# Two chained decoder blocks on one core: state outputs of the RWKV blocks in column halves, a norm's rate in three steps, the step sizes' softplus in later rounds, and the convolution split into lagged parts

## Chip, cores and metric

One core of a Trainium2 chip runs the whole program. The metric is the device time of one execution in microseconds (us). Engines are named as in the profile: PE (TensorE, matmuls; PEld is its loading of weights), DVE (VectorE), ACT (ScalarE), POOL (GpSimd), SP (SyncE, which issues the weight DMAs).

## What is computed

The reference runs two blocks behind each other on x of 256 tokens by 2048 features, all in float32. The change touches the second block's mixer alone:

```
u = rms_norm(h, norm1_g)                 # h is the first block's output after its final norm
P = u @ w_in                             # z, xbc, dt_raw, and the RWKV part pr
pr = pr + (prev - pr) * mu               # token shift
y_ssd:  xbc = silu(causal_depthwise_conv(xbc, w[4], b)); dt = softplus(dt_raw + dt_bias)
        chunked state space scan over x, B, C with dt and A
y_rwkv: S_t = S_{t-1} * w_t + (S a_t) b_t + v_t k_t ;  y_t = S_t r_t   per head of 64
h = h + concat(y_ssd, y_rwkv) @ w_out
```

There are 32 heads of 64 for each of the two mixers, so two heads share the 128 partitions. The convolution runs over 24 tiles of 128 channels (16 of x, 8 of B and C).

## The kernel before

Activations lie feature-major: a tile is 128 features by T = 256 tokens. Every large matrix product (`linear`) reads weights as float32 from HBM in pieces of 128x1024. ACT copies a piece to its rounded high part (L2036), DVE subtracts for the low part (L1199), and PE runs three matmuls for each 128x128 block (hi by hi, hi by lo, lo by hi: L703, L704, L705). Four buffers hold cut pieces. A tile of the second block's input projection has 16 blocks, hence two pieces.

Every engine runs a program of its own, in order. All are written by generators of the same shape, and the order is set by hand by where they `yield`. `second_mixer` makes rounds: in each round `main` advances by 5 yields (5 of a tile's 16 blocks), and then each of the other generators by one yield, in the order heads of even number (`heads(0)`), of odd number (`heads(1)`), `tails`, `afters`, and those of `early`. `AFTER, PAIRS, ROUNDS = 25, 56, 20` say in which round the pair's preparation begins, in which the first blocks begin, and how many rounds lie between pairs.

- `main` runs `L_sm` (4 tiles: decay, a and gate low-rank parts, and dt), then eight groups of `L_krv` (6 tiles each: k, r, v of a pair of head tiles), from the fifth on with a small gate product `L_g2` in between, then `L_bc` (8 tiles) and `L_x` (6 and 10 tiles), whose tiles go through the convolution. DVE's `raw_shift` takes a tile out of its bank (L1615), ACT scales it (L2274), DVE adds the shifted part (L1625).
- `both_rates` is in `early`. DVE makes the rate of the first block's final norm and of the second block's first norm in one round (L1259 to L1270, two reciprocals among them), ACT takes the roots (L2523, L2524). DVE then scales h in eight rounds (L1277); ACT stores h (L2528) 13 rounds in and eight rounds later loads `w2` and `a2` (L2532, L2533) into h's place.
- `steps_dt`, also in `early`, is the softplus of dt and its running sum on 32 partitions: L1646 to L1680 on DVE, two `Exp` on ACT (L2297, L2300). Its temporaries are the scratch tiles `scr[0:4]`, which `prep` uses afterwards; ACT's `prep(0)` and `prep(1)` therefore wait for its end (`dt_v["cs"]`).
- `after(b)` is `prep` of two head tiles side by side (`flight`), one `yield`, and `solve(b)`: PE multiplies (L933), DVE sorts the result with eight instructions (L1752) and transposes (L1756), and POOL inverts the 32x32 triangles by 31 pairs of instructions (L2710, L2714). DVE's `finish(b)` (L1735, L1737) waits for POOL; it is called by `solve(b+1)` or by the first block that needs it.
- `block(i, hf)` takes ten rounds: transposes (L948 to L951), masks (L958, L960 on PE, L1774 on DVE), L965, L972, then L978 to L984, L990 with L1795 on DVE, and four chunks of 32 tokens, one for each round. A chunk waits for the state of the one before (DVE L1802, ACT L2376), adds its output to bank A by one matmul with the 128x128 block-diagonal state, 32 columns wide (L1002), and makes the next state by six matmuls of 64 output columns, in pairs for the two heads (L1006, L1008, L1011). The two heads' results go to the two halves of the partitions, `HALVES`.
- `tail(i)` is the group norm of a finished head tile; it waits for `solve` to have left banks 2 and 3 (`wkv_v["xa", ...]`).
- `conv4(t)`, in `main`: DVE takes the tile out of its bank (L1851), ACT makes bias plus last tap (L2400), DVE adds three taps (L1855, three instructions), ACT applies Silu (L2403), all for the same t. Ahead of `L_bc` ACT waits until the gated output of pair 4 is stored (L2394, semaphore `st_y[1]`).

`Lag(L, f0, f1, ...)` is a helper that calls at tile t the parts in the order f_n(t - n), ..., f1(t - 1), f0(t); `tail()` runs what is left over. `timed((n, g))` starts g after n rounds.

## Time and profile before

| | |
|---|---|
| median of 3 runs | 3125.03 us (3124.04 to 3125.74) |
| the profiled execution: time | 3126.62 us |
| its span on the core | 3124.5 us |
| PE busy | 2925.9 us, 94% |
| DVE, ACT, POOL busy | 2132.1, 1559.1, 714.7 us |
| mean granted clock of PE | 0.978 |

The time and the span of the profiled execution differ by 2.1 us. "Busy" is the union of an engine's instructions; matmuls overlap, so PE's progress is better read from the starts of its instructions. The second mixer's rounds lie between about 1184 and 2035 us of the span.

### The profile page before, as it was taken

The numbers are of one execution on the slowest core, as the hardware profiler recorded it, in microseconds if no ns is written. First come the engines' busy times: TensorE is split into PE (matmuls) and PEld (weight loads), VectorE is DVE, ScalarE is ACT, GpSimd is POOL, SyncE is SP. The second block draws the span as 40 slices with busy tenths as digits, with TensorE's granted clock in tenths as the row PEclk, the third lists the DMA queues.
The fourth block names the chain that finished last, engine by engine and source line by source line (L and its number), as shares of the span: only waits on it lengthen the run. The fifth ranks groups of instructions, "written<-read, shape, count | busy, mean of one in ns | idle before, by whom it ended". The sixth has DMA issues, their size and how long they took to land. (4 is left out here: it accounts for less than half of the span.)

```text
span 3124.5 us, 51838 instructions
## 1 busy us (share of the span) xinstructions
PE 2925.9 (94%) x20742; PEld 2613.5 (84%) x20742; DVE 2132.1 (68%) x3449; ACT 1559.1 (50%) x2582; POOL 714.7 (23%) x885
## 2 busy tenths in 40 slices
PE   4976999999999998899999989998999999999998
PEld 4865998888888887888888778987888888888887
DVE  7787887775777657677777666666756665566655
ACT  3445555553555544455555555455444444444443
POOL 5256402210111100565555440000100110001100
PEclk9987999999999999999999999999999999999999
DMA  4420555556555555322222222344455555655554
GB/s 179 166 68 26 164 177 190 192 173 193 206 191 189 166 173 184 132 96 89 89 89 89 88 76 93 134 165 148 163 176 182 191 192 171 195 201 189 185 176 138
DMA packets 78958, 475.30 MB, mean 152 GB/s; under 512 B 8128, under 2 KB 11200, under 8 KB 37440
## 3 DMA queue, kind: packets, MB, share of 16 engines
q1 hardware_dynamic: 76480, 459.66, 43.1%
q10 hardware_dynamic: 2240, 12.32, 1.1%
q8 instruction: 167, 2.74, 0.4%
q14 instruction: 71, 0.58, 0.1%
HBM read 465.66 MB, written 6.29 MB: 151 GB/s over the span
## 5 line engine op out<-in xcount | busy, mean ns | idle before, releaser
L705 PE MATMUL bank<-m,m 128*128 128x256 f32 x6864 | 1931.6, 281 | 0.0
L701 PE MATMUL bank<-m,m 128*128 128x512 f32 x4736 | 1658.3, 394 | 5.3 <-DVE m L1945 2.8
L1199 DVE TENSOR_TENSOR m<-m,m 128x1024 fp32r<-128x1024 f32 (+1 forms) x944 | 1079.5, 1151 | 605.8 <-ACT m L2036 599.8
L705 PEld LDWEIGHTS bank<-m,m 128*128 128x128 f32 x6864 | 1302.1, 190 | 1.2
L2036 ACT ACTIVATE m<-m 128x1024 fp32r<-128x1024 f32 (+1 forms) x944 | 911.5, 979 | 719.8 <-PE bank L705 701.0
L701 PEld LDWEIGHTS bank<-m,m 128*128 128x128 f32 x4736 | 890.5, 188 | 204.0 <-issue 5.6
L703 PE MATMUL bank<-m,m 128*128 128x256 f32 x2128 | 639.8, 301 | 66.8 <-DVE m L1199 60.5
L704 PE MATMUL bank<-m,m 128*128 128x256 f32 x2128 | 606.5, 285 | 0.0
L703 PEld LDWEIGHTS bank<-m,m 128*128 128x128 f32 x2128 | 411.3, 193 | 96.3 <-issue 79.6
L704 PEld LDWEIGHTS bank<-m,m 128*128 128x128 f32 x2128 | 411.8, 193 | 1.8
L2691 POOL TENSOR_TENSOR m<-m,m 128x256 fp32r<-128x256 f32 x44 | 63.4, 1441 | 690.1 <-ACT m L2258 690.1
L2714 POOL TENSOR_TENSOR m<-m,m 128x31 f32<-128x31 f32 (+15 forms) x248 | 167.5, 675 | 19.5
L2710 POOL TENSOR_TENSOR m<-m,m 128x31 f32<-128x31 f32 (+15 forms) x248 | 161.3, 651 | 19.4
L2682 POOL TENSOR_TENSOR m<-m 128x256 f32<-128x256 f32 x44 | 32.6, 742 | 447.3 <-DVE m L1587 447.3
L2274 ACT ACTIVATE m<-m,m 128x256 f32<-128x256 f32 (+1 forms) x52 | 26.5, 509 | 140.9 <-DVE m L1615 140.9
L2241 ACT ACTIVATE m<-bank 128x256 f32<-128x256 f32 x88 | 34.1, 387 | 116.2 <-PE bank L705 116.1
L2685 POOL TENSOR_TENSOR m<-m,m 128x256 fp32r<-128x256 f32 x44 | 63.4, 1441 | 123.2 <-ACT m L2235 123.2
L2771 POOL TENSOR_TENSOR m<-m,m 128x256 fp32r<-128x256 f32 x8 | 7.5, 968 | 328.0 <-ACT m L2460 328.0
L717 PE MATMUL bank<-m,m 128*128 128x256 f32 x236 | 65.0, 389 | 11.7 <-ACT m L2058 11.3
L1592 DVE TENSOR_TENSOR m<-m,bank 128x256 f32<-128x256 f32 x88 | 37.1, 421 | 56.6 <-ACT m L2241 56.6
L2215 ACT ACTIVATE m<-bank 128x256 f32<-128x256 f32 x88 | 34.0, 386 | 74.9 <-PE bank L705 74.9
L2376 ACT ACTIVATE m<-bank,m 64x64 f32<-64x64 f32 x128 | 39.5, 308 | 52.4 <-PE bank L1011 40.8
(368 smaller groups left out, 2929.2 us busy)
## 6 DMA issues: line engine op xcount, KB each, us to landing
m<-in_w_up SPq DMA_DIRECT2D x88, 1024.0 KB, 4.8
m<-in_w_down SPq DMA_DIRECT2D x128, 704.0 KB, 4.1
m<-in_w_gu SPq DMA_DIRECT2D x88, 1024.0 KB, 4.8
m<-in_w_out SPq DMA_DIRECT2D x48, 1024.0 KB, 5.1
m<-in_w_krv SPq DMA_DIRECT2D x48, 1024.0 KB, 4.8
m<-in_w_xbc SPq DMA_DIRECT2D x24, 1024.0 KB, 4.8
m<-in_w_z SPq DMA_DIRECT2D x16, 1024.0 KB, 4.8
m<-in_w_in SPq DMA_DIRECT2D x14, 1024.0 KB, 4.8
```

The costliest lines, as they stand in the source:

```text
L701: pe.matmul(bank.rearrange("p (a b) -> p a b", a=2), hi, x, start=kc == L.k0, stop=False)
L703: pe.matmul(ps, hi, x[:, 0, :], start=kc == L.k0, stop=False)
L704: pe.matmul(ps, hi, x[:, 1, :], start=False, stop=False)
L705: m = pe.matmul(ps, lo, x[:, 0, :], start=False, stop=last)
L717: pe.matmul(banks[N.bank][:, 0:T], ones, square_of(N, i), start=i == 0, stop=i == N.nk - 1).then_inc(*norm_pe(("sq", q)))
L1199: v.tensor_tensor(lo_of(k), raw_of(k)[0], hi_of(k).bitcast(F32), SUB).then_inc(*lo_v(("lo", k)))
L2036: a.activation(hi_of(k), src, ACT.Copy).then_inc(*hi_a(("hi", k)))
L2376: a.activation(sn[R, R], bB[R, R], ACT.Copy, scale=PL[R, i, hf * 4 + c:hf * 4 + c + 1]).then_inc(*wkv_a(("s", i, hf, c)))
L2685: g.tensor_tensor(far[:, 1, j % 22, :], s[:, 1, :], far[:, 0, j % 22, :].bitcast(F32), SUB).then_inc(*ffn_g(("lo", j)))
L2691: g.tensor_tensor(far[:, 1, j % 22, :], cvs2[j % 4], far[:, 0, j % 22, :].bitcast(F32), SUB).then_inc(*ffn_g(("lo2", j)))
L2710: g.tensor_tensor(prod, XB[:, r + 1:32, r:r + 1].broadcast_to([128, n, r + 1]), XX[:, r:r + 1, 0:r + 1].broadcast_to([128, n, r + 1]), MUL ...
L2714: g.tensor_tensor(x5, x5, prod, ADD).then_inc(*wkv_g(*([("x", b)] if r == 30 else [])))
```

## The change

- PE's L1002 becomes two matmuls, for the 64 state columns of each head, which write the two halves of bank A's partitions.
- `both_rates` is spread over three rounds on DVE; on ACT it begins two rounds later, and its counts of rounds behind are one lower, so that the store of h and the loads of `w2`, `a2` come one round later.
- `steps_dt` begins in round 31 (`STEPS = 30`), with h's first three tiles as temporaries (partitions 96 to 128, once h is stored) and its input in `dt_`; ACT's `prep(0)` and `prep(1)` no longer wait for it.
- `after(b)` has one more `yield` ahead of `solve(b)` on every engine.
- The convolution becomes `convolved(L)`: DVE runs `conv4(t-1)` and then `raw4(t)`; ACT runs the Silu of t-2 (`gated`) and then bias and last tap of t (`weighted`). The wait for the store of pair 4 moves from the head of `L_bc` to the Silu of tile 22.

```diff
-AFTER, PAIRS, ROUNDS = 25, 56, 20
+AFTER, PAIRS, ROUNDS, STEPS = 25, 56, 20, 30
+        dth = [h[:, n, :] for n in range(3)]
@@ tensor: block
-                        m = pe.matmul(bA[:, Q], sb_, qb[:, Q], start=False, stop=c == 3)
+                        for R in HALVES:
+                            m = pe.matmul(bA[R, Q], sb_[:, R], qb[:, Q], start=False, stop=c == 3)
@@ after(b), on all four engines
                 yield from flight(lambda i: prep(2 * b + i), 2, 2)
                 yield
+                yield
                 yield from solve(b)
@@ vector: both_rates
                 v.reciprocal(rr, ms).then_inc(*norm_v())
+                yield
...
-                v.reciprocal(ms, rl).then_inc(*norm_v())
-                v.wait_ge(*norm_v.last)
+                v.reciprocal(ms, rl).then_inc(*norm_v(("rm",)))
+                yield
+                v.wait_ge(*norm_v["rm"])
@@ vector: steps_dt
-                a, e, w, p = (q[R, :] for q in scr[0:4])
-                for _ in range(5):
-                    yield
+                a, e, w, p = (q[R, :] for q in (dt_, *dth))
+                v.wait_ge(st_h, 16)
@@ vector: convolution
+            def raw4(t):
...
+            def conv4(t):
+                s, ps = cvb[t % 2], shp[t % 2]
+                v.wait_ge(*ssd_v["raw", t])
                 v.wait_ge(*ssd_a["id", t])
...
+            def convolved(L):
+                steps = Lag(L, raw4, conv4)
+                yield from linear(L, steps)
+                steps.tail()
@@ scalar: prep
-                a.wait_ge(*(wkv_v["prep", i - 2] if i >= 2 else dt_v["cs"]))
+                if i >= 2:
+                    a.wait_ge(*wkv_v["prep", i - 2])
@@ scalar: convolution
+            def convolved(L, dst):
+                def weighted(t):
                     a.wait_ge(*ssd_v["raw", t])
...
+                def gated(t):
+                    if t == 22:
+                        a.wait_ge(st_y[4 % 3], 16 * (4 // 3 + 1))
                     a.wait_ge(*ssd_v["conv", t])
-                    a.activation(dst(t), s, ACT.Silu).then_inc(*ssd_a(("conv", t)))
-                return done
+                    a.activation(dst(t), cvb[t % 2], ACT.Silu).then_inc(*ssd_a(("conv", t)))
+
+                steps = Lag(L, weighted, lambda t: None, gated)
@@ scalar: main
-                a.wait_ge(st_y[4 % 3], 16 * (4 // 3 + 1))
@@ scalar: both_rates
+                yield
+                yield
                 a.wait_ge(*norm_v["rc", N_two.id])
...
-                for _ in range(12):
+                for _ in range(11):
                     yield
@@ vector and scalar
-            second_mixer(main(), block, tail, after, steps_dt(), both_rates(...), ...)
+            second_mixer(main(), block, tail, after, timed((STEPS, steps_dt())), both_rates(...), ...)
```

## Rows read from the trace of the kernel before

**Rows 1.** Page, part 1: busy time, share of the span, instructions.
```profile
PE 2925.9 (94%) x20742; PEld 2613.5 (84%) x20742; DVE 2132.1 (68%) x3449; ACT 1559.1 (50%) x2582; POOL 714.7 (23%) x885
```
**Rows 2.** Windows of the second mixer's stages: length, busy by engine, granted clock, DMA.
```profile
1180.00:1247.00 67.00, 53.46 (x401) 51.71 (x400) 52.06 (x90) 30.28 (x43) 5.95 (x11) 0.95 0.49 168
1247.00:1334.00 87.00, 71.66 (x583) 69.28 (x582) 61.89 (x108) 41.17 (x64) 48.52 (x67) 0.94 0.36 131
1334.00:1757.00 423.00, 410.19 (x4037) 365.24 (x4035) 295.64 (x605) 242.40 (x489) 248.08 (x382) 0.98 0.27 91
1757.00:1965.00 208.00, 186.60 (x1808) 165.88 (x1809) 133.23 (x268) 112.12 (x210) 41.12 (x64) 0.96 0.26 88
```
**Rows 3.** Windows at one stall of PE and just behind it.
```profile
1464.00:1466.00 2.00, 0.32 (x3) 0.11 (x2) 1.97 (x5) 0.00 (x0) 0.00 (x0) 1.00 0.00 0
1466.80:1470.20 3.40, 3.40 (x18) 3.40 (x17) 2.60 (x5) 2.04 (x4) 0.00 (x0) 0.50 0.85 308
```
**Rows 4.** Timeline of ACT in the opening: start, length, instruction, idle before.
```profile
1189.99 0.42 ACT L2523 ACTIVATE m<-m 128x256 f32<-128x256 f32 x1 [4.66 <-DVE m L1270]
```
**Rows 5.** Timeline of DVE in the opening.
```profile
1191.70 1.23 DVE L1199 TENSOR_TENSOR m<-m,m 128x1024 fp32r<-128x1024 f32 x1 [1.74 <-ACT m L2036]
```
**Rows 6.** Timeline of PE in the opening.
```profile
1193.07 0.36 PE L703 MATMUL bank<-m,m 128*128 128x256 f32 x1 [1.70 <-DVE m L1199]
```
**Rows 7.** Groups of DVE, 1184.7 to 1240: busy, mean ns, idle before.
```profile
L1666 DVE TENSOR_TENSOR m<-m,m 32x256 f32<-32x256 f32 x8 | 3.4, 422 | 0.3
L1668 DVE TENSOR_SCALAR m<-m 32x256 f32<-32x256 f32 x8 | 3.3, 409 | 0.3
```
**Rows 8.** DMA issues, 1220 to 1250: size, us to landing.
```profile
m<-in_a ACTq DMA_DIRECT2D x1, 768.0 KB, 9.0
```
**Rows 9.** Timeline of POOL, begin of `solve(0)`.
```profile
1274.85 0.95 POOL L2703 MEMSET m<- 128x1024 f32 x1 [45.53 <-DVE m L1756]
```
**Rows 10.** Timeline of DVE where it takes up `solve(0)`'s result.
```profile
1326.51 1.25 DVE L1735 STREAM_TRANSPOSE m<-m 128x1024 f32<-128x1024 f32 x1 [4.04 <-POOL m L2714]
```
**Rows 11.** POOL's 31 additions, 1274 to 1327.
```profile
L2714 POOL TENSOR_TENSOR m<-m,m 128x31 f32<-128x31 f32 (+15 forms) x31 | 23.8, 768 | 2.4
```
**Rows 12.** The same, 1477 to 1524.
```profile
L2714 POOL TENSOR_TENSOR m<-m,m 128x31 f32<-128x31 f32 (+15 forms) x31 | 19.4, 627 | 2.4
```
**Rows 13.** Timeline of PE: a first chunk, which has no L1002.
```profile
1348.64 0.28 PE L705 MATMUL bank<-m,m 128*128 128x256 f32 x1
...
1349.01 0.29 PE L1008 MATMUL bank<-m,m 128*64 128x64 f32 x4
```
**Rows 14.** Timeline of PE: a chunk with L1002 behind a linear block.
```profile
1623.83 0.28 PE L705 MATMUL bank<-m,m 128*128 128x256 f32 x1
...
1624.37 0.29 PE L1008 MATMUL bank<-m,m 128*64 128x64 f32 x4
1624.48 0.29 PE L1011 MATMUL bank<-m,m 128*64 128x64 f32 x4
```
**Rows 15.** Timeline of PE: a chunk with L1002 behind matmuls of half width.
```profile
1378.92 0.44 PE L984 MATMUL bank<-m,m 128*64 128x128 f32 x4
...
1379.79 0.29 PE L1008 MATMUL bank<-m,m 128*64 128x64 f32 x4
```
**Rows 16.** Timeline of DVE around `solve(3)`.
```profile
1473.37 2.53 DVE L1752 TENSOR_TENSOR m<-bank,m 32x128 f32<-32x128 f32 x8
...
1480.10 0.87 DVE L1795 TENSOR_TENSOR m<-bank,m 64x256 f32<-64x256 f32 x2
```
**Rows 17.** Timeline of PE, the chunk that needs this L1795.
```profile
1482.68 0.41 PE L1002 MATMUL bank<-m,m 128*128 128x32 f32 x2
```
**Rows 18.** Timeline of ACT at the head of `L_bc`.
```profile
1767.60 1.06 ACT L2036 ACTIVATE m<-m 128x1024 fp32r<-128x1024 f32 x1 [5.20 <-DMA ysave<-m]
```
**Rows 19.** Groups of ACT, 1761 to 2030.
```profile
L2403 ACT ACTIVATE m<-m 128x256 f32<-128x256 f32 x24 | 10.0, 418 | 31.8 <-DVE m L1855 31.8
```
**Rows 20.** Groups of DVE, 1761 to 2030.
```profile
L1855 DVE SCALAR_TENSOR_TENSOR m<-m,m,m 128x255 f32<-128x255 f32 (+2 forms) x72 | 35.9, 499 | 20.6 <-ACT m L2400 18.9
```

More of the change, by code:

```diff
@@ L1839, in gated @@
                 v.tensor_tensor(VV(t), VV(t), bank_of(L_g2[t // 2], t), MUL).then_inc(*wkv_v(("gate", t)))
-            def conv4(t):
-                s, ps = cvb[t % 2], shp[t % 2]
+            def raw4(t):
+                ps = shp[t % 2]
                 L = L_x[t >= 6] if t < 16 else L_bc
@@ L1866, in main @@
                 yield from linear(L_g2[4], gated)
-                yield from linear(L_bc, conv4)
+                yield from convolved(L_bc)
                 yield from linear(L_g2[5], gated)
                 for k in range(2):
-                    yield from linear(L_x[k], conv4)
+                    yield from convolved(L_x[k])
                     yield from linear(L_g2[6 + k], gated)
@@ L1996, in vector_program @@
             v.tensor_scalar(omka, WR("rwkv_k_a_2"), -1.0, 1.0, MUL, ADD).then_inc(*once_v(("omka",)))
-            second_mixer(main(), block, tail, after, steps_dt(), both_rates(ffn_v.last),
+            second_mixer(main(), block, tail, after, timed((STEPS, steps_dt())), both_rates(ffn_v.last),
                          timed((CLOSING, chain(turn_dt(), turn_cb(), turn_x(0, 13)))))
@@ L2293, in steps_dt @@
                 R = slice(96, 128)
-                for _ in range(5):
-                    yield
+                yield
                 a.wait_ge(*dt_v["w"])
-                a.activation(scr[1][R, :], scr[2][R, :], ACT.Exp).then_inc(*dt_a(("e",)))
+                a.activation(dth[0][R, :], dth[1][R, :], ACT.Exp).then_inc(*dt_a(("e",)))
                 for _ in range(6):
@@ L2417, in main @@
                 a.wait_ge(*wkv_v["out", 9])
-                a.wait_ge(st_y[4 % 3], 16 * (4 // 3 + 1))
-                yield from linear(L_bc, conv4(L_bc, lambda t: bc[:, t - 16, :]))
+                yield from convolved(L_bc, lambda t: bc[:, t - 16, :])
                 yield from gated(5)
@@ L2422, in main @@
                 for k in range(2):
-                    yield from linear(L_x[k], conv4(L_x[k], lambda t: xT[:, t, :]))
+                    yield from convolved(L_x[k], lambda t: xT[:, t, :])
                     yield from gated(6 + k)
@@ L2427, in after @@
                 yield from flight(lambda i: prep(2 * b + i), 2, 2)
+                yield
                 yield
@@ L2521, in both_rates @@
             def both_rates():
+                yield
+                yield
                 a.wait_ge(*norm_v["rc", N_two.id])
@@ L2533, in both_rates @@
                 a.dma_start(a2s[0:96, :], d["a2"]).then_inc(ld_a2, 16)
-            second_mixer(main(), block, tail, after, steps_dt(), both_rates())
+            second_mixer(main(), block, tail, after, timed((STEPS, steps_dt())), both_rates())
             last_mixer(chain(linear(L_z, z_done), linear(L_outr, lambda t: None)), quad, iter(range(3)), norm_ssd,
@@ L2744, in after @@
                 yield from flight(lambda i: iter(range(7)), 2, 2)
+                yield
                 yield
```

14 lines of the change are left out of this document (8 added, 6 removed).

## Prediction

> **What bounds the kernel now.** I began with the page's busy shares [rows 1]: PE works 94% of the span, so an edit counts only if it shortens PE's own work or one of PE's waits. Then I cut the span into windows. In the two feed-forward parts PE is busy throughout; PE's idle time lies in the mixers, and the change touches the second one. There [rows 2] PE idles 67.0 - 53.5 = 13.5 us in the opening (1180 to 1247), 87.0 - 71.7 = 15.3 us up to the first blocks (to 1334), 12.8 us in the 423 us of steady rounds, and 21.4 us in the 208 us in which the convolution runs beside the last blocks. The same rows show a second price: the granted clock's mean is 0.94 to 0.98. [rows 3] show how that comes: PE, at 2.4 GHz, works 0.32 of 2 us, and in the 3.4 us from its restart it is granted 0.50, the level of 1.2 GHz. So such a stall costs 3.4 x 0.5 = 1.7 us more. Over rows 2 the lost clock is 0.05 x 67 + 0.06 x 87 + 0.02 x 423 + 0.04 x 208 = 25 us. In all, 63 us of idling and 25 us of clock can be had or made worse.
>
> **Opening: the rate in three rounds, softplus out of the way.** Now ACT sits 4.66 us in front of its root, waiting for DVE's six instructions [rows 4], and only then copies the next piece; DVE cuts it at 1191.70 [rows 5], and PE waits 1.70 us for it [rows 6]. After the change ACT copies that piece first, and DVE cuts it right behind its second reciprocal, about 1189.5: this stall goes. The root is needed for the first tile all the same and comes only 1.1 us earlier, so most of the next stall stays. Behind it DVE has 12.7 us of softplus between the cuts: eight pairs of 3.4 + 3.3 us [rows 7] and some 6 us of single instructions. I walked through the 26 rounds with those gone, a tile being 16 x 3 matmuls at 0.118 us = 5.7 us of PE: three stalls remain, each where ACT changes tables for a Tanh or Sigmoid ahead of a copy. PE is through the second tile at 1194.1, the third's first piece is cut at 1196.6 (2.5 us); through the fourth at 1208.1, with the fifth's piece at 1210.4 (2.3); through the fifth at 1216.1, with the sixth's at 1217.6 (1.5). From there tiles of 5.7 us follow without a stall, and PE reaches round 26 about 12 us earlier, with two half-clock stretches saved.
>
> Not all of it lasts. `w2` and `a2` are asked for one round later while PE arrives earlier; `a2` takes 9.0 us to land [rows 8], and from round 22 to round 26 PE needs 4 rounds of 1.8 us = 7.1 us. So PE waits about 2 us where it now waits 0.2. And `solve(0)` on POOL sets the pace next: it begins at 1274.85 [rows 9], ends at 1326.5, 51.7 us later, and DVE waits 4.04 us for it [rows 10], PE 5.5 us. What PE saves between these two points only lengthens that wait. The path is: opening, preparation, `solve(0)`, first blocks. On it are 12 saved, 2 lost to `a2`, 1.8 lost because `solve(0)` begins a round later, 1 for softplus instructions now between preparation and `solve(0)`, and 1.8 won back because `finish(0)` also comes a round later in the program, so that PE has done one more round when it stops. That makes 9. The 7 us of softplus that fall beside POOL's chain are covered by the wait of 4.0 us and by what is left of PE's 4 us wait in front of L933, which the extra yield relieves; without that cover they would cost up to 7.
>
> POOL's chain itself can suffer: its 31 additions take 768 ns each here, but 627 ns beside steady rounds [rows 11, 12], 4 us on the path already. The softplus adds some 7 us to the 62 us in which DVE is busy there [rows 2]; in proportion that is 0.5 us more for POOL, and I count it in the 1 us above. The Trainium skill (SBUF — State Buffer, Terms) says that of DVE and GpSimd the loser blocks for the other's whole instruction; the slower additions agree, and by it alone the eight products of 0.42 us could hold POOL for up to 3.4 us. For the opening: 9 us, from 3 (`a2`'s landing and the bursts at twice their price, little cover left) to 13.
>
> **State outputs in halves.** L1002 is one float32 matmul of two passes with the whole array, amid groups that use it in halves. A chunk without it takes 0.37 us from the last linear matmul to L1008 [rows 13], with it 0.54 [rows 14]. As halves it becomes another pair of groups like its neighbours: L1008 to L1011 is 0.11 us [rows 14], so 0.48, a gain of 0.05 for some 60 chunks, 3 us. Behind L984 [rows 15] the path L984 to L1008 is 0.87 us, because the array changes from halves to whole and back; all in halves it should be 0.22 (L984's four passes of 128 columns, half of them at a time: twice the 0.11 of the 64 columns in [rows 14]) + 0.11 + 0.11 = 0.44. That is 0.42 us for 15 chunks, 6.3 us. The 37 chunks behind other whole-array matmuls gain 0.03 to 0.2 each, 3 us. Together 12 us of PE. Bounds: if the two halves do not run beside each other, the group takes 0.22 instead of 0.11 and 112 chunks give back 12 us, which leaves nothing; if 32 columns take half of what 64 take, 0.055, it is 18 us. PE has short waits on DVE in each period of 20 rounds, and three quarters should come through: 9 us, range 3 to 14.
>
> A rule speaks against it. The Trainium skill (TensorEngine Tiling (Array Packing), Performance Considerations) warns not to take the tiling from a dimension that is already small, as each matmul has some 60 cycles of overhead; 32 moving columns are such a case. No row here has 32 columns in halves. By the page's figure, 25 ns at 2.4 GHz, two more passes in 112 chunks would be an estimated 6 us of cost in place of the gain.
>
> **`solve` a round later, in every period.** Steady rounds do not need it: PE has no stall at L933 there. DVE's burst of transposes and L1752 (about 5.3 us, [rows 16] show its middle) moves from round 95 to 96 of a period, next to the DVE work of round 97. L1795 ended at 1481.0 and PE needed it at 1482.68 [rows 16, 17]; the burst a round later (3.9 us later, minus 1.2 us of cutting that now comes ahead) ends L1795 at about 1482.9. With the tail's square and root behind it I expect 0.5 to 1 us of new waits, six times: 4 us lost, range 0 to 12 (with a stretch of half clock in half of the periods).
>
> **Convolution.** Queued behind ACT's Silu are its copies and the blocks' evacuations. ACT waits 31.8 us for L1855 before 24 Silus, 1.3 each [rows 19], and DVE 18.9 us for ACT before L1855 [rows 20]. After the change both find their input a tile old. The wait for the store, 5.2 us of ACT [rows 18], goes entirely: the Silu of tile 22 comes seven tiles later. That store alone explains two PE stalls of 2.8 and 1.4 us and one stretch of half clock: 5.9 us. The rest of the 21.4 us and of the clock (8 us) is 24 us, mostly PE waiting for ACT behind a Silu. Against it: `conv4(t-1)` now stands ahead of `raw4(t)` on DVE, 3 x 0.5 = 1.5 us, so where DVE is late the tile leaves its bank 1.5 us later and ACT gains 0.9 instead of 2.4 us. I take 60%: 14 us. Bank turnover is safe, as PE has the other bank's tile (5.7 us) in between; the last Silu of each run still waits, three times. Sum 20 us, range 8 to 27.
>
> **Sum.** 9 + 9 - 4 + 20 = 34 us off the profiled execution's 3126.6, 3092.6; the median of the runs is 1.6 lower, so 3091.
>
> **Rivals.**
> - *Given back.* POOL's chain and `a2` take the opening's gain, new waits in the periods take that of the halves, and the convolution yields its lower half: about -14 us, 3111. For it speaks that DVE is busy 62 of 87 us beside POOL [rows 2].
> - *Everything runs.* With stalls gone the clock stays up: 13 + 14 - 0 + 27 = 54 us, 3071. Against it: the burst in `prep` that stalls PE at 1465.9 [rows 3] is untouched.
> - *Small columns.* The halves do not overlap at 32 columns, and the pair of groups costs the 0.22 us of the bound above: the 9 us are gone, 3100. For it: the passes of the two halves are too short to hide each other's weights; against it: the neighbours with 64 columns do [rows 14]. The Trainium skill's tiling rule above is this case.
> - *No effect.* DVE is late in every tile and ACT waits for L1851 as long as it did for L1855; PE's stalls change places. 3122 to 3128.
> - *Slower.* The later burst in `solve` stalls PE not for 0.5 but for 5 us in each of seven periods, and each stall brings a stretch of half clock: 7 x (5 + 1.7) = 47 us against 38 gained, 3134. It decides from 3.7 us of stall per period on, where the 38 us are used up. Against it: the old timeline leaves 1.7 us of room.
>
> **Chances.** As forecast (3078 to 3104) 0.56; given back 0.16; everything 0.10; small columns 0.06; no effect 0.05; slower 0.07. The range that leaves out no more than 2 in 10 is 3074 to 3112; the likeliest case's own is 3078 to 3104. Within 0.2% (6.2 us, about what a measurement of this kernel can tell from no change): 0.05; faster 0.88; slower 0.07.
>
> **What would show it.** In the profile after: ACT's wait in front of L2523 shorter and PE's wait for L1199 in the opening about 6 us in place of 13.5; a wait of some 2 us for `in_a`; DVE's wait for POOL in front of its first L1735; L984 to L1008 at 0.44 us; waits of PE on L1795 near each `solve`; no idle ACT before Silu. Wrong it would be if these DVE bursts stall PE for whole microseconds, or if ACT's wait simply moves to L1851's successor.

## Result and the profile after

The changed kernel takes 3108.84 us (median of 4 runs, 3107.23 to 3113.15) against 3125.39 us before (4 runs). The ratio is 0.9947, with an interval of 0.9936 to 0.9959: 16.5 us faster. The forecast was 34 us, so the direction was right and about half of the gain was missing. Two of the four terms of the sum came out at their number, two did not.

The profiled execution took 3113.15 us, with a span of 3111.1 us. First the stages of the second mixer, as windows of the changed kernel. The columns are those of [rows 2]. The first inner cut lies at the same round as before. The second lies at round 61, where [rows 2] cut at round 58.8, and the last two lie at the same times as before, not at the same rounds.

```profile
1180.00:1236.00 56.00, 52.19 (x409) 51.15 (x408) 39.03 (x63) 27.84 (x39) 5.67 (x11) 0.97 0.61 205
1236.00:1343.00 107.00, 85.50 (x630) 81.00 (x630) 81.22 (x142) 47.62 (x75) 53.75 (x77) 0.90 0.33 116
1343.00:1757.00 414.00, 390.61 (x4071) 345.04 (x4070) 286.02 (x590) 231.84 (x468) 239.31 (x360) 0.98 0.25 88
1757.00:1965.00 208.00, 195.68 (x2040) 174.68 (x2038) 144.09 (x289) 116.40 (x225) 47.87 (x76) 0.97 0.28 99
```

PE's idle time in the opening is 3.8 us in place of 13.5. In the second stage it is 21.5 us at a granted clock of 0.90, where [rows 2] show 15.3 us at 0.94, and where the same rounds before (1247.0 to 1341.2) take 94.2 us in place of 107.2: the gain of the first stage is gone there. In the last row, where the convolution runs, PE is busy 195.7 us in place of 186.6.

To see where time came and went I counted rounds in each trace by the starts of PE's L704 (L703 before), five of them to a round, and took how much sooner than before each kernel reached a round. All values are counted from its own round 1, one profiled execution each:

| kernel | round 26 | 31 | 61 | 78 | 160 | 190 | 220 | last block |
|---|---|---|---|---|---|---|---|---|
| changed | 12.5 | 8.8 | -0.5 | -2.0 | -5.6 | -0.5 | 10.5 | 14.9 |
| changed, no extra yield | 12.3 | 11.5 | 4.3 | 4.7 | 10.3 | 23.4 | 31.3 | 35.9 |
| changed, L1004 whole | 12.7 | 12.4 | 3.8 | 3.8 | -1.6 | 1.7 | 6.1 | 10.6 |
| changed, softplus from round 61 | 12.7 | 12.8 | 11.6 | 2.6 | -0.9 | 5.8 | 13.7 | 18.2 |
| changed, `finish` a round earlier | 12.5 | 12.5 | 4.5 | 5.3 | 2.4 | 13.7 | 20.2 | 24.8 |
| changed, transpose a round later | 12.5 | 11.5 | 2.1 | 0.9 | 6.0 | 18.3 | 26.3 | 31.0 |
| no extra yield, softplus from 45 | 12.5 | 11.2 | 3.5 | 2.4 | 10.5 | 23.6 | 31.5 | 36.0 |
| no extra yield, softplus from 203 | 12.7 | 11.6 | 11.0 | 11.6 | 19.7 | 32.7 | 36.8 | 41.3 |
| before + rates alone | 0.9 | 0.9 | 0.9 | 0.9 | 1.0 | 1.0 | 1.0 | 1.1 |
| before + softplus alone | 9.9 | 3.9 | -5.0 | -5.0 | -3.4 | -0.5 | 0.9 | 1.1 |
| before + halves alone | 0.0 | -0.3 | 0.2 | 0.7 | 6.1 | 7.6 | 12.9 | 13.4 |
| before + yield alone | -0.1 | 0.0 | -1.2 | -1.4 | -8.4 | -12.8 | -12.9 | -12.7 |
| before + convolution alone | -0.1 | -0.5 | 0.1 | 0.1 | 0.3 | 12.1 | 16.4 | 20.9 |

Between rounds 26 and 61 one program does not always take the same time: the changed kernel, the one with a whole L1004 and the one with `finish` moved run the same instructions up to the first blocks, and stand at -0.5, 3.8 and 4.5 in round 61. So a value in column 61 is good to some 4 us, and the changed kernel's own profile shows a poor pass. Most of the difference arises between rounds 26 and 31, where PE waits 2.2 us for the load of `a2` in the changed kernel's pass and 0.2 us or less in the other two (rows below).

**The opening.** The timeline of ACT and of DVE in the changed kernel, and PE's largest stall there:

```profile
1192.43 0.42 ACT L2548 ACTIVATE m<-m 128x256 f32<-128x256 f32 x1 [4.67 <-DVE m L1275]
```
```profile
1190.90 1.16 DVE L1202 TENSOR_TENSOR m<-m,m 128x1024 fp32r<-128x1024 f32 x1
```
```profile
1197.99 0.55 PE L704 MATMUL bank<-m,m 128*128 128x256 f32 x1 [2.29 <-DVE m L1202]
```

ACT's wait did not shrink (4.67 us, [rows 4] 4.66): it only came behind the copy. The cut is at 1190.90 without a wait of its own, and PE's 1.70 us of [rows 6] are gone. PE reaches round 26 12.5 us sooner. The step of the prediction that walked through these rounds said 12.

**What followed the opening.** The load of `a2`, POOL's start of `solve(0)`, and DVE where it takes up the result:

```profile
m<-in_a ACTq DMA_DIRECT2D x1, 768.0 KB, 12.6
```
```profile
1238.76 1.06 PE L908 MATMUL bank<-m,m 96*128 96x256 f32 x2 [2.19 <-DMA m<-in_a]
```
```profile
1275.97 0.95 POOL L2728 MEMSET m<- 128x1024 f32 x1 [54.77 <-DVE m L1760]
```
```profile
1329.24 1.24 DVE L1739 STREAM_TRANSPOSE m<-m 128x1024 f32<-128x1024 f32 x1
```

The wait for `a2` is the 2 us that the step on `a2` gave it, but it costs more than itself. These are rounds 26 to 31 as windows of the changed kernel, of run 11 (the same instructions there) and of run 12:

```profile
1234.63:1250.19 15.56, 13.37 (x93) 12.49 (x92) 6.04 (x14) 8.33 (x15) 0.00 (x0) 0.89 0.59 207
```
```profile
1234.52:1246.45 11.93, 11.69 (x93) 11.30 (x92) 5.98 (x14) 8.10 (x15) 0.00 (x0) 1.00 0.68 255
```
```profile
1234.91:1252.77 17.86, 14.71 (x94) 13.82 (x92) 6.07 (x14) 8.36 (x15) 0.00 (x0) 0.81 0.48 174
```

PE waits 2.2, 0.2 and 3.1 us for `in_a` in them, and the granted clock is 0.89, 1.00 and 0.81. So the wait of 2.2 us costs 3.6 in this pass, before softplus has begun: its first instruction stands at 1254.99, and round 31 begins at 1250.19.

POOL begins at 1275.97, not sooner than the 1274.85 of [rows 9], although PE was 11 us ahead at round 26 by the clock of the two traces. (Round 1 itself begins at 1182.21 here and at 1180.73 before. Counted from there POOL begins at 93.8 us, before at 94.1.) And in front of L1739 there is no wait in brackets, where [rows 10] show 4.04 us for POOL: DVE comes to it late, and the cover on which the step counted is not there.

**State outputs.** Two chunks on PE in the changed kernel, the first behind the half-width L985, the second behind a linear block:

```profile
1382.80 0.44 PE L985 MATMUL bank<-m,m 128*64 128x128 f32 x4
1383.02 0.31 PE L1004 MATMUL bank<-m,m 128*64 128x32 f32 x4
...
1383.25 0.34 PE L1010 MATMUL bank<-m,m 128*64 128x64 f32 x4
```
```profile
1357.63 0.28 PE L706 MATMUL bank<-m,m 128*128 128x256 f32 x1
1357.84 0.31 PE L1004 MATMUL bank<-m,m 128*64 128x32 f32 x4
...
1358.12 0.29 PE L1010 MATMUL bank<-m,m 128*64 128x64 f32 x4
```

L1010 is the old L1008. Behind L985 it starts 0.45 us after it (0.87 in [rows 15], forecast 0.44); behind the linear matmul 0.49 us after (0.54 in [rows 14], forecast 0.48). Over all chunks without a wait in the traces of the kernel before and of run 15, the path from the last matmul ahead of the state output to this one fell by 0.42 us behind L984 (15 chunks), by 0.03 behind a linear matmul (60 chunks), by 0.08 and 0.03 behind L965 and L972 (15 each) and by 0.22 behind L960 (7). That is 11 us of PE, 6.3 of them behind L984.

**Steady rounds.** The chain of the extra yield around `solve(3)` in the changed kernel: DVE's timeline, ACT's, and PE's.

```profile
1481.03 2.52 DVE L1756 TENSOR_TENSOR m<-bank,m 32x128 f32<-32x128 f32 x8
1483.59 1.25 DVE L1760 STREAM_TRANSPOSE m<-m 128x1024 f32<-128x1024 f32 x1
1484.86 0.42 DVE L1620 TENSOR_TENSOR m<-bank,m 128x256 f32<-128x256 f32 x1
```
```profile
1485.32 0.51 ACT L2287 ACTIVATE m<-m,m 128x256 f32<-128x256 f32 x1 [6.29 <-DVE m L1620]
1485.74 1.04 ACT L2049 ACTIVATE m<-m 128x1024 fp32r<-128x1024 f32 x1
1486.81 0.60 ACT L2364 ACTIVATE m<-bank 128x512 f32<-128x512 f32 x1
```
```profile
1487.46 0.49 PE L959 MATMUL bank<-m,m 64*128 64x128 f32 x4 [1.30 <-ACT m L2364]
```

The burst is not what PE waits for. It stands ahead of L1620, which takes a linear tile out of its bank; ACT idles 6.29 us for that tile, and behind it in ACT's order stands L2364, the evacuation of a block's transposes, for which PE waits.

**Convolution.** Groups of DVE and ACT in the changed kernel, 1757 to 2025:

```profile
L1862 DVE SCALAR_TENSOR_TENSOR m<-m,m,m 128x255 f32<-128x255 f32 (+2 forms) x72 | 36.7, 510 | 3.6 <-ACT m L2416 1.8
```
```profile
L2423 ACT ACTIVATE m<-m 128x256 f32<-128x256 f32 x24 | 9.9, 411 | 3.4 <-DVE m L1862 3.1
```

ACT's idle time before Silu fell from 31.8 us to 3.4 [rows 19], DVE's before its three taps from 20.6 to 3.6 [rows 20]. Two further rows of ACT belong to it. The bias and last tap, in the changed kernel and before:

```profile
L2416 ACT ACTIVATE m<-m,m 128x256 f32<-128x256 f32 x24 | 14.4, 601 | 64.3 <-DVE m L1855 64.2
```
```profile
L2400 ACT ACTIVATE m<-m,m 128x256 f32<-128x256 f32 x24 | 14.4, 600 | 48.2 <-DVE m L1851 48.2
```

So 16 of the 28 us came back as a longer wait for the tile to leave its bank. And ACT's loads of its function table ahead of Silu, in the changed kernel and before:

```profile
L2423 ACT ACT_TABLE_LOAD x4 | 5.1, 1283 | 0.1
```
```profile
L2403 ACT ACT_TABLE_LOAD x7 | 9.0, 1283 | 0.1
```

Those ahead of the tails' root (L2399, before L2386) fell from 6 to 3 as well: together 7.7 us less of ACT's own time, which no term of the prediction names.

### The profile page after: what moved, and what is told of

It is laid out like the page before. It is cut to its first block and busy times, and to the rows that moved or that the text cites. A ratio compares the mean times of both kernels' runs of the same rounds, so it can differ in the third digit from the quotient of the medians.

```text
span 3111.1 us, 52307 instructions
## 1 busy us (share of the span) xinstructions
PE 2913.5 (94%) x20966; PEld 2599.6 (84%) x20966; DVE 2131.0 (68%) x3449; ACT 1550.0 (50%) x2575; POOL 717.1 (23%) x885
## 3 DMA queue, kind: packets, MB, share of 16 engines
HBM read 465.66 MB, written 6.29 MB: 152 GB/s over the span
## 5 line engine op out<-in xcount | busy, mean ns | idle before, releaser
L2049 ACT ACTIVATE m<-m 128x1024 fp32r<-128x1024 f32 (+1 forms) x944 | 911.6, 979 | 716.4 <-PE bank L706 701.9
L704 PE MATMUL bank<-m,m 128*128 128x256 f32 x2128 | 640.2, 301 | 61.6 <-DVE m L1202 51.5
L704 PEld LDWEIGHTS bank<-m,m 128*128 128x128 f32 x2128 | 412.5, 194 | 88.4 <-issue 73.6
L2287 ACT ACTIVATE m<-m,m 128x256 f32<-128x256 f32 (+1 forms) x52 | 26.5, 510 | 164.3 <-DVE m L1620 164.3
L718 PE MATMUL bank<-m,m 128*128 128x256 f32 x236 | 64.8, 388 | 11.8 <-ACT m L2071 11.3
L2389 ACT ACTIVATE m<-bank,m 64x64 f32<-64x64 f32 x128 | 39.6, 310 | 51.4 <-PE bank L1013 36.9
```

The source lines that it names most:

```text
L704: pe.matmul(ps, hi, x[:, 0, :], start=kc == L.k0, stop=False)
L718: pe.matmul(banks[N.bank][:, 0:T], ones, square_of(N, i), start=i == 0, stop=i == N.nk - 1).then_inc(*norm_pe(("sq", q)))
L2049: a.activation(hi_of(k), src, ACT.Copy).then_inc(*hi_a(("hi", k)))
L2389: a.activation(sn[R, R], bB[R, R], ACT.Copy, scale=PL[R, i, hf * 4 + c:hf * 4 + c + 1]).then_inc(*wkv_a(("s", i, hf, c)))
```

## Experiments

Each run's own comparison has kernel-before runs on the same chip; their median lay between 3125.8 and 3126.9 us, for the changed kernel's own 3125.39. Differences from the changed kernel are those of the medians as they stand; against their own kernels before they would be up to 1.5 us different. "Theory" and "rival" are those of the expectation above each result.

**1. Without the extra yield.**

```diff
 def after(b):        # on all four engines
     yield from flight(lambda i: prep(2 * b + i), 2, 2)
     yield
-    yield
     yield from solve(b)
```


> The changed kernel without the extra yield in front of solve, on every engine; all else as changed. Theory A (the gain was lost in two places, and this is one): with the yield, DVE's burst of two transposes and eight sorts stands in front of the evacuation L1620, ACT idles 6.3 us in front of L2287, its copy L2364 comes late and PE waits 1.3 us at L959, plus 1.9 us at L1004 behind L1806, some 2.4 us in each of about six periods; without it those waits fall back to about 2.5 us per period and the time falls by 8 to 14 us, to about 3098 us. Rival B (the yield costs what was forecast or less, and the gain of the halves was never there): within 4 us of the changed kernel, 3105 to 3109. Rival C (the yield relieved the first solve, PE at L934, and was worth it): slower than the changed kernel by 2 to 5 us.

3091.58 us, ratio 0.9886 (0.9874 to 0.9899): 17 us faster than the changed kernel. Theory A is right in its place and too low in size: it expected 8 to 14 us, and the waits at L959 below, 8.4 us fewer, are half of what came. The list of PE's waits, of the changed kernel and of this one (us in total, times, longest):

```profile
PE bank L959 <- ACT m L2364: 11.6, 7, 2.8
```
```profile
PE bank L959 <- ACT m L2362: 3.2, 2, 2.3
```

**2. State output whole again.**

```diff
-for R in HALVES:
-    m = pe.matmul(bA[R, Q], sb_[:, R], qb[:, Q], start=False, stop=c == 3)
+m = pe.matmul(bA[:, Q], sb_, qb[:, Q], start=False, stop=c == 3)
```


> The changed kernel with L1004 as one matmul of the whole array again; all else as changed. Theory A (the halves are sized right, 11 us of PE's own time over 112 chunks, and three quarters come through): slower than the changed kernel by 7 to 11 us, 3116 to 3120 us. Rival B (the waits on DVE and ACT in the steady rounds took it all): within 2 us, 3107 to 3111. Rival D (the halves cost, as narrow tiles would): faster than the changed kernel by 2 us or more.

3119.69 us, ratio 0.9975 (0.9966 to 0.9985): 10.9 us slower than the changed kernel (9.7 by the kernels before of each). Theory A; rivals B and D fall.

**3. Softplus in the steady rounds.**

```diff
-AFTER, PAIRS, ROUNDS, STEPS = 25, 56, 20, 30
+AFTER, PAIRS, ROUNDS, STEPS = 25, 56, 20, 60
```


> The changed kernel with STEPS 60 in place of 30: softplus in rounds 61 to 73, where a round takes 3 to 4 us and DVE is idle for about 1 us of each; all else as changed. Theory A (in rounds 31 to 44 DVE is busy without a pause, so the 7 us of softplus and the slowdown beside POOL delay its cuts and evacuations, and PE loses 11 us between round 26 and round 65): 6 to 11 us faster than the changed kernel, about 3100. Rival E (POOL's chain of 51 us sets the end of the first solve whatever DVE does in front of it): within 2 us of the changed kernel. Rival F (softplus is no better in the later rounds, its stalls only move): within 3 us either way, with new waits of PE in rounds 61 to 73.

3111.34 us (3107.22 to 3122.92), ratio 0.9958 (0.9943 to 0.9974), no better than the changed kernel: theory A missed. Its first half holds, as PE reaches round 61 11.6 us ahead. But PE then loses 9.0 us up to round 78, where softplus now stands, at L1004 in

```profile
1344.10 0.31 PE L1004 MATMUL bank<-m,m 128*64 128x32 f32 x4 [1.39 <-DVE m L1806]
```

and others like them. That was rival F. The trace also shows POOL's chain as a limit, rival E's point. POOL begins 11.7 us sooner than in the changed kernel (9.3 when each is counted from its own round 1, of which 3.7 are rounds 26 to 31, with the wait for `a2`, rather than softplus), and now both DVE and PE wait (POOL, then DVE, then PE):

```profile
1264.31 0.96 POOL L2728 MEMSET m<- 128x1024 f32 x1 [45.46 <-DVE m L1760]
```
```profile
1314.85 1.25 DVE L1739 STREAM_TRANSPOSE m<-m 128x1024 f32<-128x1024 f32 x1 [6.33 <-POOL m L2739]
```
```profile
1323.87 1.12 PE L966 MATMUL bank<-m,m 128*128 128x64 f32 x4 [11.24 <-DVE m L1778]
```

**4. Convolution alone**, in the kernel before: the part of the change's diff with `raw4`, `conv4`, `convolved`, `weighted` and `gated`, and nothing else.

> The kernel before with the convolution's parts lagged alone (raw4, conv4 on DVE; bias and Silu on ACT; the wait for the store at tile 22). Theory A (this part gave what was forecast, 19 to 20 us between round 180 and the end): 3103 to 3108 us, 17 to 22 us faster than before, so more than the whole change gives. Rival G (its gain is owed to the other parts, halves above all, which make room on PE): 8 to 13 us faster, 3112 to 3117.

3106.62 us, ratio 0.9933 (0.9921 to 0.9945): 20.0 us faster. Theory A. PE's wait of 2.8 us at L948, which the prediction put down to the store, is not in this trace.

**5. Softplus beside POOL's chain.** Run 1 with `STEPS` 44.

```diff
-AFTER, PAIRS, ROUNDS, STEPS = 25, 56, 20, 30
+AFTER, PAIRS, ROUNDS, STEPS = 25, 56, 20, 44
```


> The changed kernel without the extra yield and with STEPS 44: softplus in rounds 45 to 57, beside POOL's chain of 51 us and nothing of the preparation. The last run with softplus out of rounds 31 to 44 kept PE 18.6 us ahead of before until round 58 and then stood 11.2 us for the first solve, and lost 9 us more in rounds 61 to 78, where softplus was. Theory A (softplus costs PE its full DVE time wherever PE depends on DVE, and is free only where PE must wait for POOL in any case): PE reaches round 61 about 12 to 14 us ahead of before in place of 1.7, and the time is 8 to 12 us under that of the run without the yield, 3080 to 3084 us. Rival E (POOL's chain is slowed by it, or DVE's queue holds back something else that the first blocks need): within 3 us of that run, 3089 to 3094.

3090.19 us, ratio 0.9882 (0.9867 to 0.9898), against 3091.58 in run 1: rival E. POOL does begin early (1263.57), but PE falls from 12.5 us ahead at round 26 to 3.5 at round 61. In the rounds before 45 it keeps its lead (11.2 us in round 31 and in round 45), so the loss lies where softplus is. So also this place, which by the prediction was covered, costs.

**6. Without the series.** Run 1 with the eight pairs L1670, L1672 of softplus left out, so dt is not the softplus of its input.

```diff
 for k in range(7, -1, -1):
-    v.wait_ge(*dt_v.last)
-    v.tensor_tensor(p, p, w, MUL).then_inc(*dt_v())
-    v.wait_ge(*dt_v.last)
-    v.tensor_scalar(p, p, cf[k], None, ADD).then_inc(*dt_v())
     yield
```


> The changed kernel without the extra yield, with the eight pairs of softplus's series left out (so dt is not the reference's): some 6.7 us of DVE's time in rounds 35 to 44 less, all else where it was. Theory A (these instructions, not the rounds to which the rate was spread or the later loads, cost the stretch from round 26 to 58): PE is 8 to 12 us further ahead at round 58 than with them, and the whole is 6 to 11 us faster than the run without the yield, 3081 to 3086. Rival H (the stretch is lost to DVE's normal work, which now starts late against the slowed POOL side, or to the load of a2): under 3 us faster.

3085.53 us, 6.0 us under run 1 by the medians, at the low end of theory A. The two profiles show less: 5.8 against 4.3 us ahead at round 61, 37.4 against 35.9 at the end. Taken alone this run is no more than a hint.

**7. Rates alone**, in the kernel before.

```diff
 v.reciprocal(rr, ms).then_inc(*norm_v())            # DVE, both_rates
+yield
...
-v.reciprocal(ms, rl).then_inc(*norm_v())
-v.wait_ge(*norm_v.last)
+v.reciprocal(ms, rl).then_inc(*norm_v(("rm",)))
+yield
+v.wait_ge(*norm_v["rm"])
```
(and two more yields on ACT ahead of the roots, one less behind them)

> The kernel before with the rates alone spread over three rounds, and the store of h and the loads of w2 and a2 one round later; softplus stays in rounds 6 to 18. Theory A (most of the opening's 12 us came from softplus leaving it; the split saves the stall in front of L1199 at 1193 alone, 1.7 us and its stretch of half clock, and the later load of a2 takes 0 to 2 back): 0 to 3 us faster than before, 3123 to 3127. Rival I (the split itself gave the larger part of the opening): 5 us or more faster.

3125.18 us, ratio 0.9992 (0.9984 to 1.0001): 1.7 us, theory A, though no change at all is inside the interval too.

**8. The extra yield alone**, in the kernel before: the edit of run 1 the other way round.

> The kernel before with the extra yield in front of solve alone. Theory A (the yield costs by itself, through DVE's burst in front of L1615 and ACT behind it, not through an interplay with the other parts): 12 to 20 us slower than before, 3138 to 3146. Rival J (it costs only where halves have shortened PE's rounds, or only the relief at L933 of the first solve shows): within 6 us of before.

3140.46 us, ratio 1.0045 (1.0033 to 1.0056): 13.6 us slower. Theory A. PE's waits in that kernel, and in the kernel before:

```profile
PE bank L958 <- ACT m L2353: 13.4, 9, 3.5
```
```profile
PE bank L958 <- ACT m L2351: 4.8, 4, 1.9
```

These are 8.6 us more of the same wait; the remaining 5 us were not traced to single rows. In the changed kernel one part of such a remainder can be seen: from 1790 to 1812, with a 2.78 us wait at L959 (1799.55) in it, PE is granted 0.77; without the extra yield it is granted 1.00 from 1770 to 1812.

```profile
1790.00:1812.00 22.00, 18.99 (x150) 16.66 (x152) 15.09 (x32) 7.74 (x15) 14.56 (x26) 0.77 0.15 48
```

**9. Softplus in rounds 203 to 215.** Run 1 with

```diff
-AFTER, PAIRS, ROUNDS, STEPS = 25, 56, 20, 30
+AFTER, PAIRS, ROUNDS, STEPS = 25, 56, 20, 202
-dth = [h[:, n, :] for n in range(3)]
+dth = [h[:, 13 + n, :] for n in range(3)]
```


> The changed kernel without the extra yield and with STEPS 202, softplus in rounds 203 to 215 beside the last two head tiles, where nothing of a preparation or a solve is left and DVE is idle for 0.8 to 1.3 us of each round (its three temporaries in the h tiles 13 to 15, which are written later than 0 to 2). Theory A (softplus costs wherever DVE is behind PE or its order holds up the blocks; here it would not): PE is 10 to 13 us ahead of before in round 61, keeps it, and loses 0 to 4 us from round 203 to 216; time 3080 to 3086 us. Rival K (the saved time is taken by DVE's other work in rounds 41 to 60 and by POOL's chain, as in the run with softplus in rounds 45 to 57): 3087 to 3091.

3086.70 us, ratio 0.9875 (0.9862 to 0.9889): the fastest complete kernel here, 4.9 us under run 1, though the intervals touch. By the medians it lies between the two expectations, 0.3 us under rival K's bound. Its trace bears out theory A up to round 200: 11.0 us ahead in round 61, and kept. But from 200 to 220 it loses 1.6 us where run 1 gains 4.2. So softplus costs 5.8 us here too, more than the 0 to 4 expected. The windows from round 26 to 65 in this kernel and in run 5:

```profile
1234.00:1343.30 109.30, 93.05 (x761) 88.22 (x759) 73.28 (x125) 51.26 (x83) 66.18 (x93) 0.94 0.35 125
```
```profile
1233.00:1349.70 116.70, 96.43 (x760) 90.63 (x760) 89.10 (x152) 54.69 (x87) 68.02 (x94) 0.91 0.34 117
```

The same rounds take 7.4 us more with softplus in them, and DVE is busy 89.1 - 73.3 = 15.8 us more.

**10. Extra yield in front of the first solve alone**, otherwise as run 9.

```diff
 yield
+if b == 0:
+    yield
 yield from solve(b)
```


> As the run before, but the extra yield stands in front of the first solve alone. With the yield everywhere and softplus away PE was 18.6 us ahead at round 58 and stood 11.2 us for POOL; without the yield and with softplus in rounds 45 to 57 it was 4.7 us ahead. Theory A (the yield hurts in the steady rounds alone; in front of the first solve it relieves PE at L934 and the chain of POOL sets the end either way): within 3 us of the run without any extra yield, either side. Rival L (the first solve wants it, as its POOL chain begins no later and PE gets a round more done before it stops): 3 us or more faster.

3088.77 us, ratio 0.9879 (0.9866 to 0.9893), within 2.1 us of run 9. Theory A: the yield's cost lies in the later solves.

**11. `finish` a round earlier**, in the changed kernel.

```diff
 def solve(b):        # DVE
-    yield
     if b > 0:
         finish(b - 1)
+    yield
     v.wait_ge(*wkv_pe["sol", b])
```


> The changed kernel with DVE's finish(b-1), a transpose and a copy of together 1.8 us, in front of the yield in solve instead of behind it: it stays in the round in which it was before the change, and only the eight sorts and the last transpose come a round later. Theory A (the extra yield costs because the whole burst of 5.3 us stands in front of the evacuation L1620, behind which ACT's L2287, L2049 and L2364 and then PE's L959 wait): PE's waits at L959 of 1.3 us and their stretches of half clock go, and the time is 5 to 12 us under the changed kernel's 3108.8, 3097 to 3104. Rival M (the yield costs because the solve ends a round later for what follows it, POOL's chain or the tail's banks): within 3 us of the changed kernel.

3103.20 us, ratio 0.9926 (0.9913 to 0.9938): 5.6 us under the changed kernel, within theory A's range, but its reason was not met. PE's wait at L959 stays, at 1.06 us, and over the steady rounds and the last blocks (1343 to 1965) it is 10.3 us in seven where the changed kernel has 11.6 in seven. DVE's timeline says why: the sorts L1756 did not move up by the 1.8 us that were taken away, because they wait for PE's L934, which is itself a round later.

```profile
1472.87 2.52 DVE L1756 TENSOR_TENSOR m<-bank,m 32x128 f32<-32x128 f32 x8 [1.07 <-PE bank L934]
...
1476.70 0.42 DVE L1620 TENSOR_TENSOR m<-bank,m 128x256 f32<-128x256 f32 x1
```

**12. Softplus alone**, in the kernel before: its input in `dt_`, temporaries in h, from round 31 on.

> The kernel before with softplus alone moved to round 31, into the h tiles. Theory A (its DVE time is given back in the rounds in which it is put, since DVE and not POOL or PE sets the pace there): PE gains 8 to 10 us up to round 26, loses 8 to 12 from there to round 61, and the time is within 4 us of before. Rival E (POOL's chain covers it, as forecast): 5 to 9 us faster than before, 3118 to 3122.

3127.54 us, ratio 1.0006 (0.9996 to 1.0015): no gain. Theory A by the time. But its reason holds for a part alone. PE gains 9.9 us up to round 26, then waits 3.1 us for `a2` and is granted 0.81, and is 3.9 us ahead in round 31 (at 1252.77), before softplus's first instruction at 1257.54. From there to round 61 it loses 8.9 us more, so rival E, which is the prediction's own cover, falls all the same. POOL begins its first chain at

```profile
1274.53 0.95 POOL L2703 MEMSET m<- 128x1024 f32 x1 [53.52 <-DVE m L1756]
```

which, counted from round 1 of each trace, is 0.6 us later than before (94.7 against 94.1).

**13. The transpose behind the sorts a round later**, in the changed kernel.

```diff
-v.wait_ge(*wkv_v.last)
+yield
+v.wait_ge(*wkv_v[("xa", b, 1)])
 v.transpose(XB..., XA...).then_inc(*wkv_v(("xb0", b)))     # L1760
```


> The changed kernel, extra yield and all, with DVE's last instruction of solve, the transpose L1760 of 1.25 us, one round later than the eight sorts. In the run with finish a round earlier DVE then waited 1.07 us for PE's L934 itself, so the sorts began only a little earlier, ACT still idled 5.8 us in front of L2287, and PE still waited 1.06 us at L959. Theory A (what counts is everything that DVE does between L934 and the evacuation L1620; L2287, L2049 and L2364 follow it on ACT, and L959 waits for L2364): with 1.25 us less in between, L959's wait of 1.30 us falls to 0.0 to 0.2 in each period with its stretch of half clock, and the time falls to 3094 to 3102 us. Rival M (the yield costs because what follows the solve is later, POOL's chain above all, which now begins a round later still): the time rises by 2 us or more, with waits of DVE on POOL.

3097.17 us, ratio 0.9905 (0.9892 to 0.9919): 11.7 of the 17 us come back with the extra yield still in place. DVE goes from the sorts straight to L1620, and PE starts L959 without a wait in the same place:

```profile
1475.24 2.53 DVE L1756 TENSOR_TENSOR m<-bank,m 32x128 f32<-32x128 f32 x8
1477.80 0.42 DVE L1620 TENSOR_TENSOR m<-bank,m 128x256 f32<-128x256 f32 x1
```
```profile
1480.39 0.49 PE L959 MATMUL bank<-m,m 64*128 64x128 f32 x4
```
```profile
PE bank L959 <- ACT m L2365: 3.9, 2, 2.3
```

POOL's chain now hangs on a transpose that comes a round later in the program (by the traces `solve(3)`'s chain starts at 1482.3 here and at 1484.9 in the changed kernel, which is further behind by then), and in this kernel's list of DVE's waits from 1354 to 1812 POOL is not named. Rival M falls.

**14. Both of these edits.**

> Both edits together: finish one round earlier and the transpose L1760 one round later than in the changed kernel, so only the eight sorts (2.5 us) are left in the round of L934. Theory A: no wait at L959 in the steady rounds, and 3 to 6 us under the run with finish alone moved (3103.2), 3092 to 3100 us; what is left of the 17 us then lies with L1004 and the later rounds. Rival M: no better than 3101.

3098.78 us, ratio 0.9909 (0.9896 to 0.9923): inside theory A's range, but no better than run 13. With all but 3.7 us of L959's wait gone, as in run 13, the earlier `finish` had nothing left to give.

**15. Halves alone**, in the kernel before.

> The kernel before with L1002 alone in halves. Theory A (as in the changed kernel, where taking the halves back cost 10.9 us): 7 to 12 us faster than before, 3114 to 3119. Rival B (in the kernel before, PE's waits on DVE in each period take part of it): 3 to 6 us faster.

3116.39 us, ratio 0.9968 (0.9957 to 0.9979): 9.6 us, theory A.

## Why the prediction was half right

Alone in the kernel before the parts give 20.0 (convolution), 9.6 (halves), 1.7 (rates), -1.7 (softplus) and -13.6 (yield), together 16.0 us; the whole change gave 16.5. The match is closer than the parts are: without the yield the rest gains 35.0 us (3126.58 to 3091.58), of which convolution and halves alone make 29.6, so within the change the opening is worth some 5 us, and the yield costs some 18 (35.0 against 16.5). These two differences cancel.

- **State outputs: right.** 9 forecast, 9.6 alone and 10.9 within the change. The two paths, 0.44 and 0.48 us, came out at 0.45 and 0.49, and PE's own gain of 12 us at 11. The Trainium skill (TensorEngine Tiling (Array Packing), Performance Considerations) warns against taking the tiling from a dimension that is already small. The prediction held the 32 moving columns to be such a case, but the edit halves the 128 state columns and leaves the 32 as they are, so the warning isn't put to the test; the 6 us of cost that the prediction estimated from the page's overhead per matmul did not show. More than half of PE's gain, 6.3 of 11 us, lies in the 15 chunks behind L984, where whole-array matmuls no longer stand between half-width groups; the 60 chunks behind a linear matmul, which is whole-array itself, give 1.6.
- **Convolution: right in number, in part by luck.** 20 forecast, 20.0 measured. The waits before Silu and for the store went as forecast. But the prediction took 60% of the remaining 24 us as a flat share. 16 of ACT's 28 us before Silu came back before the bias, and six table loads, 7.7 us of ACT, went that no term had. No run separates the two.
- **Opening: 9 forecast, about 0 alone and some 5 us within the change without the yield.** The walk through the 26 rounds (12 us) was right. `a2` was set down as a wait of 2 us and nothing behind it; the profiles with this opening show 0 to 2.2 us, and the longest of them cost 3.6. The step that failed is the cost of softplus behind them: "1 for softplus instructions now between preparation and `solve(0)`", and "the 7 us of softplus that fall beside POOL's chain are covered". The prediction's path should have put POOL at 1274.85 - 12 + 2 + 1 + 1.8 = 1267.65, 86.9 us behind round 1. It began 93.8 us behind round 1 in the changed kernel and 90.1 in run 11, with the same code up to there; with softplus away, in run 3, 84.4. Less what rounds 26 to 31 took more than in run 3 (3.7 and 0.1 us), softplus cost some 5.6 us up to POOL's start in both, where 1 was set down. The stated price without cover, up to 7 us, is what run 5 shows for the rounds beside POOL: 12.5 - 3.5 = 9.0 us lost from round 26 to 61, against 12.7 - 11.0 = 1.7 in run 9, so 7.3. Neither cover was real. DVE's 4.0 us wait on POOL was room for a DVE that arrives when it did before; with the lead of the opening it had more to do in the same time.
- **`solve` a round later: 4 forecast, 13.6 alone and 17 to 18.5 within the change.** Here the step looked at the wrong consumer. It followed the burst to L1795 and PE's need of it, and expected all of the new waits there. None came: PE's waits for this instruction (now L1799) are 2.8 us in six with the extra yield and 2.8 in six without it, and were 3.3 in six before. (The sum there has a slip too: 1481.0 + 3.9 - 1.2 is 1483.7, not 1482.9.) It didn't follow what else stands behind the burst on DVE, the evacuation L1620, and what stands behind that on ACT. Runs 11 and 13 show the chain: L934, sorts, transpose, L1620, L2287, L2049, L2364, L959. It is the work between L934 and L1620 that counts: 1.25 us less of it (run 13) gave 11.7 us back over all periods, while 1.8 us less ahead of L934 (run 11) left the wait standing.

What is open: the 5.6 us that run 11 did gain. Between rounds 160 and 190 it gained 11.3 us where the changed kernel gained 5.1, and its profile had the better pass at `a2` (3.6 us in rounds 26 to 31). Which of the two makes the difference of the medians I can't say; nor how often the wait for `a2` is long, as each kernel has one profile. Nor is the 5 us by which the parts' waits fall short of run 8's loss assigned row by row.

Where should softplus be, then? Its cost by place, from the table, in which a difference can carry some 4 us of the passes' own: 9.9 us in rounds 6 to 18 (before against run 12), (12.3 - 4.3) - 1.7 = 6.3 in 31 to 44 (run 1 against 9), 7.3 in 45 to 57 (run 5), 9.0 - 1.5 = 7.5 in 61 to 78 (run 3 against the changed kernel), 5.8 in 203 to 216 (run 9 against 1). It is 12.7 us of DVE's time in the opening and 15.8 beside POOL, and PE paid 5.8 to 9.9 for it in each place. Moving it is worth a few us, no more. Leaving out its series, some 6 to 9 us of DVE's time, gave 6.0 us in run 6, moving the whole of it to round 203 gave 4.9; whether shortening beats moving is not shown.

## What to carry to other kernels

An engine's wait is room for added work only if the engine would still arrive early once everything in front of it has sped up: work that leaves a bottleneck stage and lands on the same queue two stages later is the same work. When a burst is delayed, list everything behind it on its engine, and then everything behind those instructions on theirs. The consumer that hurts can be two engines away from the burst, and one transpose moved out of the gap can be worth more than the edit that needed the gap. Ask of a load's wait what the clock does behind it, and look at more than one pass before a loss is put down to the work that comes next: 3.6 us of what looked like softplus's cost stood before its first instruction. And test each part alone in the old kernel: here one of five was giving back nearly half of what the others won.

## What the runs showed of the hardware

Beside POOL's chain it was DVE that got slower. Where POOL does nothing, softplus's products take 422 ns and its additions 290 (run 9, the first fence). In the changed kernel the means are 525 and 449. The timelines of DVE and POOL show how, at the last pair:

```profile
L1669 DVE TENSOR_TENSOR m<-m 32x256 f32<-32x256 f32 x8 | 3.4, 422 | 0.3
L1671 DVE TENSOR_SCALAR m<-m 32x256 f32<-32x256 f32 x8 | 2.3, 290 | 0.3
```
```profile
1289.42 0.71 DVE L1670 TENSOR_TENSOR m<-m 32x256 f32<-32x256 f32 x1
1290.17 0.58 DVE L1672 TENSOR_SCALAR m<-m 32x256 f32<-32x256 f32 x1
```
```profile
1289.13 0.72 POOL L2739 TENSOR_TENSOR m<-m,m 128x207 f32<-128x207 f32 x1
1289.93 0.66 POOL L2735 TENSOR_TENSOR m<-m,m 128x220 f32<-128x220 f32 x1
```

POOL's instruction that runs when the product starts ends at 1289.85, and the product ends 0.28 us later; the next ends at 1290.59, and the addition ends 0.16 us later. The last four pairs all look like this: each stands until the POOL instruction at its side is done, 0.26 to 0.43 us, and then takes 0.28 us (a product) or 0.15 to 0.16 (an addition). The Trainium skill (SBUF — State Buffer, Terms) has the loser blocked while the other's instruction holds the ports; these rows agree, with DVE as the loser for what is left of POOL's instruction. The 409 of [rows 7] is a mean over six additions at 290 and two, beside a POOL instruction, at 977 and 553. All 16 instructions together cost 2.1 us more than in run 9, and 3.6 more in run 1, where more of them stand beside the chain (means of 620 and 544).

The prediction expected POOL to suffer by 0.5 us. It did not: its additions fell from the 768 ns of [rows 11] to 690, its products rose from 702 to 773, and the chain from its first memset to its last addition takes 51.4 us where it took 51.7.

The load of `a2`, asked for while the opening ran faster, took 12.6 us to land where [rows 8] have 9.0, 12.7 in run 12 and 10.7 to 12.2 in the other traces in which softplus had left the opening.
